# Two transformer blocks in one kernel: the first four weight units read raw weighted tokens, and VectorE makes one slot's low half

## The reference, cut to what matters

```
u = rmsnorm(h, norm_mix_pre_w[layer])      # h * rsqrt(mean(h*h) + 1e-6) * w
proj = u @ w_in[layer]
q, k, v, z, xbc, dt_raw, gate_logits = jnp.split(proj, offsets, axis=-1)
```

## Time and profile before

| | |
|---|---|
| median of 3 runs | 1797.44 us |
| profiled execution, whole | 1798.96 us |
| its span | 1797.1 us |
| PE busy | 1761.1 us, 98% |
| DVE, ACT, POOL busy | 834.1, 767.8, 786.4 us |
| first weight matmul starts | 21.19 us |
| PE idle before the constants land | 10.35 us |

### The profile page before, as it was taken

How to read it: one execution, slowest core, us unless ns; L and a number is a source line. 1 busy time by engine, 2 the same in 40 slices (tenths; PEclk the granted TensorE clock), 3 DMA queues, 4 the chain that set the end, 5 groups by cost and what they waited for, 6 DMA issues and landing times.

```text
span 1797.1 us, 24798 instructions
## 1 busy us (share of the span) xinstructions
PE 1761.1 (98%) x8958; PEld 1453.1 (81%) x8958; DVE 834.1 (46%) x1560; ACT 767.8 (43%) x1264; POOL 786.4 (44%) x607
## 2 busy tenths in 40 slices
PE   7999999999999999999999999999999999999998
PEld 5777788888888888888888888888778888888877
DVE  5554555677766311273111113899838433320044
ACT  5444654566664322353223233545555322322253
POOL 4322344433333555435444444365434544455543
PEclk9999999999999999999999999999999999999999
DMA  5112233332333222233222322232212222223321
GB/s 194 64 61 83 82 106 107 105 111 101 98 102 129 94 94 94 94 106 117 94 97 95 101 94 94 71 106 71 71 59 83 94 93 97 101 94 106 106 82 47
DMA packets 47803, 170.67 MB, mean 95 GB/s; under 512 B 5312, under 2 KB 7488, under 8 KB 47456
## 3 DMA queue, kind: packets, MB, share of 16 engines
q1 hardware_dynamic: 44352, 156.25, 26.4%
q10 hardware_dynamic: 3360, 13.17, 2.1%
HBM read 167.24 MB, written 2.16 MB: 94 GB/s over the span
## 4 chain that ended last, share of the span: by engine, by line
PE 93%; DVE 5%; ACT 1%; issue 0%; DMA 0%; SPq 0%; DVEq 0%; POOLq 0%; POOL 0%; ACTq 0%
PE bank L441 28%; PE bank L443 28%; PE bank L442 28%; DVE bank L2408 1%; PE bank L618 1%; PE bank L765 1%; PE bank L627 1%; PE bank L640 1%; DVE xs L1922 1%; PE bank L552 1%; PE bank L769 1%; DVE u_lo L1927 1%; PE bank L749 1%; PE bank L479 0%; PE bank L740 0%
## 5 line engine op out<-in xcount | busy, mean ns | idle before, releaser
L370 POOL TENSOR_TENSOR w_lo<-raw,w_hi 128x512 fp32r<-128x512 f32 x578 | 758.2, 1333 | 979.1 <-ACT w_hi L1034 979.0
L441 PE MATMUL bank<-u_hi,w_hi 128*128 128x512 f32 (+1 forms) x1624 | 624.7, 385 | 8.5 <-DVE u_lo L1927 8.2
L443 PE MATMUL bank<-u_hi,w_lo 128*128 128x512 f32 (+1 forms) x1624 | 612.3, 377 | 0.0
L442 PE MATMUL bank<-u_lo,w_hi 128*128 128x512 f32 (+1 forms) x1624 | 611.6, 377 | 0.0
L1034 ACT ACTIVATE w_hi<-raw 128x1024 fp32r<-128x1024 f32 x289 | 303.9, 1053 | 279.9 <-PE bank L443 279.5
L441 PEld LDWEIGHTS bank<-u_hi,w_hi 128*128 128x128 f32 x1624 | 305.5, 188 | 68.8 <-DVE u_lo L1927 9.4
L443 PEld LDWEIGHTS bank<-u_hi,w_lo 128*128 128x128 f32 x1624 | 305.5, 188 | 57.5
L442 PEld LDWEIGHTS bank<-u_lo,w_hi 128*128 128x128 f32 x1624 | 305.9, 188 | 53.3 <-issue 0.2
L441 PE MATMUL bank<-v_hi,w_hi 128*128 128x512 f32 (+1 forms) x368 | 133.8, 364 | 2.7 <-DVE v_lo L2493 2.7
L442 PE MATMUL bank<-v_lo,w_hi 128*128 128x512 f32 (+1 forms) x368 | 133.0, 361 | 0.0
L443 PE MATMUL bank<-v_hi,w_lo 128*128 128x512 f32 (+1 forms) x368 | 133.0, 361 | 0.0
(11 more groups left out here) (323 smaller groups left out, 2162.7 us busy)
## 6 DMA issues: line engine op xcount, KB each, us to landing
raw<-weights SPq DMA_DIRECT2D x289, 512.0 KB, 3.6
bc<-acs ACTq DMA_DIRECT2D x16, 512.0 KB, 3.7
xs<-x SPq DMA_DIRECT2D x4, 512.0 KB, 5.4
xs<-x ACTq DMA_DIRECT2D x1, 2048.0 KB, 8.1
rt<-ret_tables ACTq DMA_DIRECT2D x1, 1536.0 KB, 7.5
out<-xs SPq DMA_DIRECT2D x12, 128.0 KB, 1.8
dist<-att_tables SPq DMA_DIRECT2D x1, 512.0 KB, 10.8
p_raw<-p ACTq DMA_DIRECT2D x1, 512.0 KB, 8.3
```

Of the source, the lines that this page charges most:

```text
L370: return nc.gpsimd.tensor_tensor(w_lo[:, slot, w], raw[:, slot, w], w_hi[:, slot, w].bitcast(F32), ALU.subtract)
L441: mm(dst, w_hi[:, slot, w], hi, start=first, stop=False)
L442: mm(dst, w_hi[:, slot, w], lo, start=False, stop=False)
L443: return mm(dst, w_lo[:, slot, w], hi, start=False, stop=last)
```

## The change

Six edits, all in the first 50 us.

1. Two new tiles, `raw_hi` and `raw_lo`, hold the high and low part of `xs * weight`, the tokens without the norm's factor. ScalarE makes `raw_hi` with an Identity whose scale is the weight vector, VectorE makes `raw_lo` (`raw_rest`). The first four units (k, q, v of head pair 0, and dt) multiply these. Their read-outs move from ScalarE to VectorE (`scaled_out`), which multiplies by the factor, kept in `x_scale`.
2. Of TensorE's idle matmuls one `keep_clock(1)` stays after the sum, the `keep_clock(2)` after the spread is gone, and the spread itself moves into the pair of units, ahead of chunk 3, into bank 7.
3. The second slot's low half is made by VectorE (`second_low`, two halves), and GpSimd waits for it before it goes on with the third slot.
4. ScalarE loads the root's table ahead of the squares; `raw_high` calls stand between the splits; the splits of slots 2 and 3 come after all `raw_high` calls and both before `round_u`.
5. VectorE makes the normalised `u_hi` and `u_lo` for the other units only after `raw_lo` and the copy of the factor. The read-outs of k and q stand inside that loop after chunk 2's first step, that of v after chunk 6's, that of dt after the second `normal`.
6. TensorE waits for all eight chunks of `u` ahead of attention step 0.

```diff
-            with pool.Fori(0, ROTATED_FROM // RING) as g:
+            low_halves(0)
+            pool.wait_ge(lo_done, 2)
+            low_halves(2)
+            low_halves(3)
+            with pool.Fori(1, ROTATED_FROM // RING) as g:
...
                 for c in range(TILES):
+                    if c in between:
+                        between[c]()
                     pe.wait_ge(ready, ready0 + c + 1)
...
             keep_clock(1)
-            stat_broadcast(STATS["pre1"][1])
-            keep_clock(2)
-            unit_pair(Turn("mix"), u_hi, u_lo, u_ready, 0)
+            unit_pair(Turn("mix"), raw_hi, raw_lo, sem("raw_ready"), 0,
+                      {3: lambda: stat_broadcast(STATS["pre1"][1], ps[7])})
...
             v_turn(0)
+            pe.wait_ge(u_ready, C8)
...
+            def raw_high(c):
+                af(raw_hi[:, c, :], xs[:, c, :], ACT.Identity, scale=v("pre1", c)).then_inc(sem("raw_hi"), 1)
+
+            act.wait_ge(out_free[0], 1)
+            load_root_table()
...
+            act.wait_ge(sem("const_landed"), 32)
+            raw_high(0)
             split(0, 0)
+            split(1, 1)
+            raw_high(1)
+            raw_high(2)
             stat_root(0)
-            split(1, 1)
+            for c in range(3, C8):
+                raw_high(c)
             split(2, 2)
+            split(3, 3)
             round_u(0)
-            split(3, 3)
...
+            def raw_rest(c):
+                dve.wait_ge(sem("raw_hi"), c + 1)
+                stt(out=raw_lo[:, c, :], in0=xs[:, c, :], scalar=v("pre1", c), in1=raw_hi[:, c, :].bitcast(F32),
+                    op0=ALU.mult, op1=ALU.subtract).then_inc(sem("raw_ready"), 1)
+
+            def second_low(n):
+                w = slice(n * TILES * P // 2, (n + 1) * TILES * P // 2)
+                return tt(w_lo[:, 1, w], raw[:, 1, w], w_hi[:, 1, w].bitcast(F32), ALU.subtract)
+
+            def scaled_out(name, dst, factor=1.0):
+                job = JOBS[name]
+                dve.wait_ge(out_ready[job.bank], job.m + 1)
+                n = dst.shape[0]
+                stt(out=dst, in0=ps[job.bank][0:n, :], scalar=factor, in1=x_scale[0:n, :], op0=ALU.mult, op1=ALU.mult)\
+                    .then_inc(out_free[job.bank], 1)
+
+            def first_norm():
+                name = "pre1"
+                _, k = STATS[name]
+                raw_rest(0)
+                dve.wait_ge(hi_done, 2)
+                second_low(0)
+                def beside_root():
+                    dve.wait_ge(lo_done, 1)
+                    second_low(1).then_inc(lo_done, 1)
+                    raw_rest(1)
+                    raw_rest(2)
+                dve.wait_ge(sem("summed"), SUMMED[name] + 1)
+                factors(D, EPS, k, between=beside_root)
+                for c in range(3, C8):
+                    raw_rest(c)
+                dve.wait_ge(rb_ready, k + 1)
+                nc.vector.tensor_copy(x_scale[:], ps[7][:])
...
+                    if c == 2:
+                        scaled_out(("k", 0), k_t[0][:])
+                        scaled_out(("q", 0), q_t[0][:], -float(HEAD) ** -0.5)
+                    if c == 6:
+                        scaled_out(("v", 0), v_t[:])
                 rest(C8 - 1)
...
             for step in range(2):
                 logit(step)
                 normal(step)
+            scaled_out(("dt", 0), acs_h[:])
```

More of the change, by code:

```diff
@@ L218, in block_program @@
     att_lo = place("att_lo", [P, PAIRS, T], F32R, at=work + 20 * K)
+    raw_hi = place("raw_hi", [P, C8, T], F32R, at=work + 8 * K)
+    raw_lo = place("raw_lo", [P, C8, T], F32R, at=work + 48 * K)
     m_at = work + 32 * K
@@ L528, in apart_unit, with unit_pair @@
                 last_mm.then_inc(out_ready[j % 2], 1)
-            def unit_pair(turn, hi, lo, ready, ready0):
+            def unit_pair(turn, hi, lo, ready, ready0, between={}):
                 for j in range(2):
@@ L559, in stat_sum, with stat_broadcast @@
                 last.then_inc(sem("summed"), 1)
-            def stat_broadcast(k):
+            def stat_broadcast(k, to=rb):
                 pe.wait_ge(factor_ready, k + 1)
                 for t in range(QB):
-                    last = nc.tensor.transpose(rb[:, t * P:(t + 1) * P], tiny[:, 40 + t:41 + t].broadcast_to([P, P]), ident)
+                    last = nc.tensor.transpose(to[:, t * P:(t + 1) * P], tiny[:, 40 + t:41 + t].broadcast_to([P, P]), ident)
                 last.then_inc(rb_ready, 1)
@@ L592, in job_tiles @@
                             pe.wait_ge(sem("y_split"), Y_SPLIT.index(t) + 1)
+                    elif job.unit < RING:
+                        hi, lo = raw_hi, raw_lo
                     else:
@@ L1138, in k_in @@
                     act.wait_ge(sem("scores_ready"), 8 * (i - 1))
-                evict(("k", i), k_t[i % 2][:])
+                if i:
+                    evict(("k", i), k_t[i % 2][:])
                 refill(("k", i))
             def q_in(i):
-                evict(("q", i), q_t[i % 2][:], scale=-float(HEAD) ** -0.5)
+                if i:
+                    evict(("q", i), q_t[i % 2][:], scale=-float(HEAD) ** -0.5)
                 refill(("q", i))
@@ L1149, in v_in @@
                     act.wait_ge(sem("v_turned"), i)
-                evict(("v", i), v_t[:])
+                    evict(("v", i), v_t[:])
                 refill(("v", i))
@@ L1234, in _ @@
             exponentials(1)
-            evict(("dt", 0), acs_h[:])
             refill(("dt", 0))
@@ L1802, in sum_squares, with factors @@
                     tt(diag[:], diag[:], sq[:, c % 2, :], ALU.add).then_inc(sq_used, 1)
-            def factors(width, eps, k, input_var=None):
+            def factors(width, eps, k, input_var=None, between=lambda: None):
                 if input_var is None:
@@ L1813, in factors @@
                         op0=ALU.mult, op1=ALU.add).then_inc(var_ready, 1)
+                between()
                 dve.wait_ge(sd_ready, k + 1)
@@ L1829, in stat @@
                 dve.wait_ge(rb_ready, k + 1)
-            def pre_norm(name, n0):
-                stat(name)
+            def raw_rest(c):
[5 more added lines that the diff above has]
+                return tt(w_lo[:, 1, w], raw[:, 1, w], w_hi[:, 1, w].bitcast(F32), ALU.subtract)
@@ L1835, in rest @@
                 def rest(c):
-                    dve.wait_ge(u_hi_ready, n0 + c + 1)
-                    tt(u_lo[:, c, :], sq[:, c % 2, :], u_hi[:, c, :].bitcast(F32), ALU.subtract)\
-                        .then_inc(u_ready, 1)
+                    dve.wait_ge(u_hi_ready, c + 1)
+                    tt(u_lo[:, c, :], sq[:, c % 2, :], u_hi[:, c, :].bitcast(F32), ALU.subtract).then_inc(u_ready, 1)
                 for c in range(C8):
                     if c >= 2:
-                        dve.wait_ge(u_ready, n0 + c - 1)
@@ L1843, in pre_norm @@
-                    stt(out=sq[:, c % 2, :], in0=xs[:, c, :], scalar=v(name, c), in1=rb[:], op0=ALU.mult,
+                        dve.wait_ge(u_ready, c - 1)
+                    stt(out=sq[:, c % 2, :], in0=xs[:, c, :], scalar=v(name, c), in1=ps[7][:], op0=ALU.mult,
                         op1=ALU.mult).then_inc(n_ready, 1)
@@ L1958, in _ @@
                 dve.wait_ge(landed_x, 16)
-            pre_norm("pre1", 0)
+            first_norm()
             dve.wait_ge(sem("dist_landed"), 16)
```

## The result

The changed kernel takes 1800.96 us (median of 15 runs, 1800.45 to 1802.54), the kernel before, run beside it, 1797.56 us (15 runs). The ratio is 1.002, with a 95% interval of 1.0013 to 1.0026: slower by 3.4 us. By the bound of 0.2% (3.6 us) that the prediction set itself this still counts as the same; the interval of the ratio says that it is a small loss and not none. Forecast were 1800.2 us, with 1796.2 to 1802.5 as the range.

A forecast was written before the change was run, and what follows sets the result against it. TensorE's stream, busy 98% of the span, was taken as the bound. The early start is used up; k's second unit comes 1.9 us late, dt 2.8, so the median goes from 1797.44 to 1800.2 us; range 1796.2 to 1802.5.

The forecast's parts named there:

- The rule of turns: VectorE and GpSimd take turns at their port; four raw_lo at 1.8 us each, list done at 27.05 us.
- The other reading: raw_lo steps run undisturbed beside GpSimd; some 4.4 us would go from VectorE's list.
- The pair's end: TensorE's first pair of units, at the lower clock until 21.9 us, ends at 30.9 us; before, about 32.4.
- The early start: TensorE's pair starts at 16.9 us in place of 21.4; v then starts at 31.95 against 32.85.
- The probabilities: Attention step 0: ready at 47.3 us after ScalarE's splits, table and GpSimd's turns; k's second unit 1.9 us late.
- The clock's fall: Rival: clock falls in TensorE's 3 us stall ahead of step 0; +3.8 us, 1801.2 us; chance 0.2.
- the forecast's last step: TensorE reaches dt_turn at 50.35 us, waits for dt's read-out until 51.2, starts 2.8 us late.
- its shift: Whole span grows by 2.8 us, added to the median of 1797.44 us.
- best case of 1794.2: Faster rival: VectorE never waits for GpSimd and clock rises at once; -3.2 us. Some gain surviving had chance 0.25.

The follow-up runs named there:

- e4: Changed kernel with GpSimd's low halves of slots 2 and 3 held back until all eight raw_lo are made: 1800.80 us.
- e8: e2 with the clock raised before the pair by four idle matmuls on the first tokens and two in place of one after the sum: 1800.93 us.
- e7: e8 and e4 together, dt's read-out early: 1798.24 us.
- e11: e10 with ScalarE's exponentials of step 0 put behind the first of its three splits instead of behind all three: 1797.53 us.
- e1: Changed kernel with two idle 128x512 matmuls on TensorE in the stall ahead of attention step 0: 1801.32 us.
- e6: Changed kernel with one part undone, GpSimd making the second slot's low half again: 1802.90 us.
- second trace of before: The kernel before, unchanged, profiled once more: 1797.72 us, span 1795.9 us.
- e5: e2 with the eight u_lo of the first norm made by GpSimd and the read-outs of k, q and v moved to later chunks: 1801.38 us.
- e10: e7 with the eight u_lo of the first norm made by GpSimd as in e5: 1798.60 us.
- e13: Kernel before with the idle matmuls of e8 and GpSimd's slots 2 and 3 held back until the first u_lo: 1798.83 us.
- e2: Changed kernel with dt's read-out on VectorE moved ahead of the first normalisation of step 0: 1799.44 us.

## Why the prediction was right, and where it was off

**The rule of turns held.** The four `raw_lo` beside GpSimd's four halves took 6.86 us, 7.2 forecast, and slowed GpSimd too (6.41 us for its four, 4.94 in the earlier trace rows); the list of five ended at 26.3 us, 27.05 forecast. GpSimd's timeline:

```profile
19.37 6.41 POOL L372 TENSOR_TENSOR w_lo<-raw,w_hi 128x512 fp32r<-128x512 f32 x4 [3.34 <-ACT w_hi L1044]
```

Without GpSimd the five took 3.40 us (e4). The other reading, by which they would have run undisturbed beside it, does not hold for this kernel. The turns by themselves didn't set the time, though: by e4, k's read-out would have come only 0.5 us earlier without them.

**The pair's end and the tie.** Start 16.97 (16.9 forecast), end of the last matmul 30.93 (30.9), of k's own last one 30.25; k's read-out 30.36 (31.15); v's start 31.13 (31.95). That VectorE's list and the slow clock tie is shown by e4, e8 and e7 together. The early start of 4.5 us shrinks to 1.7 at v against the first trace of before; against the second, 3.1 us shrink to 0.6.

**The probabilities.** Forecast for 47.3, they came at 45.78, 1.5 us early. Of this 0.7 is there at the end of `raw_lo` (26.32, not 27.05) and 1.2 at the first exponential (43.16, not 44.4). The mechanism (splits, table, turns with GpSimd) is on the chain row by row; e11 took two of the splits off the way, in another start, and dt's read-out held the step up in their place. How much of the delay is the table's or the turns' is not split up further.

**The clock's fall** was a rival with 0.2, and the profiled execution has it. So the forecast's last step, a wait of 1 us for dt on TensorE, isn't in that execution: the slow matmuls took its place. Its price was foreseen as hidden in part by dt's wait; it was hidden altogether: `dt_turn` began at 50.49, VectorE's read-out ended at 50.28 (51.2 forecast). The wait itself stands in e1, e4 and e6, at 1.43 to 1.46 us. That either path ends at about the same time is why the forecast held. e1 and e8 show the unhidden price, some 1.5 us. The evidence that the prediction held against the fall was one trace, and the second trace of the same kernel has the fall there.

**The size.** By the first trace `attended(0)` came 2.06 us late (53.84 against 51.78), less than the 2.8 forecast, while the medians differ by 3.4. The term that was missing is the base: the prediction added its shift to the median, but worked it out against a trace whose start lay 1.15 us later than in the second trace of before. Against that one the shift is 3.2 us at `attended(0)` and 2.9 over the span. The time around the span grew from 1.8 us (1797.72 with 1795.9) to 2.1 (1800.92 with 1798.8). This goes with the kernel: all runs of the changed one and of e1 to e4, e7 and e8 have 2.1 to 2.2 us around the span, all of before, e5, e6, e10, e11 and e13 1.8 to 1.9. So 0.3 us of e11's lead over the changed kernel lie outside the span, and e6's loss inside it is 2.2 us, not 1.9. What makes that 0.3 us stays open. That the forecast time was this close is luck: two errors, steps up to dt's transposes taken as 0.8 us too long and a base 1.2 us too late, have opposite signs.

**The chances.** For slower, 0.2, 0.1 and a tenth of 0.45 add up to 0.35, not to 0.31 as written. Faster by over 0.2% got 0.04, from a best case of 1794.2. e7's and e11's fastest runs are 1796.58 and 1796.87 us, with k's read-out over 2 us earlier than in the changed kernel; neither comes near 1794.2.

## What to carry to other kernels

When TensorE's start is pulled forward, list what the helping engines must still deliver before it can go on, in their own order: here VectorE got three read-outs, eight `raw_lo` and two low halves ahead of work with a due time, and the gain ended at the first of these. A chain of waits shows one of two chains that tie; shorten it alone and little moves (0.5 us of 4 in e4). A read-out placed in front of a step is free only as long as that step waits for something later still.

## What the runs showed of the hardware

A VectorE step of 128x4 with its inputs in SBUF takes 0.16 us (second trace of before), or 1.15 to 1.27 if one of GpSimd's 128x512 subtractions has just begun (e13, first trace of before). Which of the two happens depends on a few tenths of a microsecond at the kernel's start, and it moved the whole kernel before by 1.15 us between two executions of the same program.

The granted clock fell to 0.50 after stalls with 0.30 and 0.18 of TensorE busy in two microseconds in one execution, and not in another kernel's with a stall of the same length (e2). It fell behind a single idle time of 1.45 us in e1 and of 1.46 in e4, and not behind one of 1.43 in e6. Behind the same 2.14 us at 1310 us it fell in one of two traces of the kernel before. So a fall can't be told from the idle time alone, and a short stall has to be priced with and without one: about 1.5 us where TensorE's stream is what the end waits for (e1, e8), little where something else is (the 2.14 us above).
